# Solving the RWKV-7 chunk systems of a hybrid backbone with 32-row instead of 64-row TensorE tiles, with the products, copies and router reordered to match

## What is computed

```python
def step(state, inp):
    r_t, w_t, k_t, v_t, a_t, b_t = inp
    sa = jnp.einsum('bhvk,bhk->bhv', state, a_t)
    state = (state * w_t[:, :, None, :] + sa[..., None] * b_t[:, :, None, :]
             + v_t[..., None] * k_t[:, :, None, :])
    return state, jnp.einsum('bhvk,bhk->bhv', state, r_t)

for d in range(2):          # forwards, then backwards
    s_ctx, y = rwkv7_scan(r_c, dec, k_d, v_c, -kk_c, kk_c * a, state0, rev)
    _, y = rwkv7_scan(r_l, dec, k_d, v_l, -kk_l, kk_l * a, s_ctx, rev)
...
logits = (h @ w_router).astype(jnp.float32)      # layer 1, before the experts
top_logit, top_idx = lax.top_k(logits, TOP_K)
```

## Time and profile before

| | before |
|---|---|
| median of 3 runs | 2844.2 us (2843.36 to 2848.82) |
| the profiled execution's own time | 2841.97 us |
| its span | 2840.2 us |
| PE busy | 2741.2 us, 97% of the span |
| DVE busy, ACT busy | 1923.5 us (68%), 1524.9 us (54%) |
| the chain that ended last, by engine | PE 90%, DVE 6%, ACT 2%, issue 1% |
| the two scans, from the first D2 stage to the first product behind them | 107.80 to 242.38 us, 1253.40 to 1390.20 us |
| the expert passes | from 1698.5 us on |

### The profile page before, as it was taken

One profiled execution on the slowest core, in us unless ns is written; L12 is line 12 of the kernel. 1 busy time (PEld: TensorE's weight loads), 2 busy tenths in 40 slices (PEclk: granted clock), 3 DMA queues, 4 the chain that ended last, 5 costly groups with the idle time before them and its releaser, 6 DMA issues.

```text
span 2840.2 us, 49672 instructions
## 1 busy us (share of the span) xinstructions
PE 2741.2 (97%) x19396; PEld 2270.1 (80%) x19396; DVE 1923.5 (68%) x2524; ACT 1524.9 (54%) x2045; POOL 0.2 (0%) x4
## 2 busy tenths in 40 slices
PE   7999999999999999899999989999999999999997
PEld 5787777887788888667878988888888888888886
DVE  3766575336322333676656669888898988889897
ACT  5534374223322222543446447777777777777775
POOL 0000000000000000000000000000000000000000
PEclk8999999999999999999999989999999999999998
DMA  6010373224222232201034439999999999999995
GB/s 272 2 47 31 107 267 111 96 100 160 75 104 92 101 123 100 75 1 47 31 134 164 179 153 357 349 346 365 353 360 358 357 348 346 365 353 361 358 357 205
DMA packets 79842, 575.81 MB, mean 203 GB/s; under 512 B 8896, under 2 KB 10176, under 8 KB 10176
## 3 DMA queue, kind: packets, MB, share of 16 engines
q1 hardware_dynamic: 78960, 568.49, 53.1%
q10 hardware_dynamic: 720, 4.99, 0.4%
HBM read 572.39 MB, written 1.05 MB: 202 GB/s over the span
## 4 chain that ended last, share of the span: by engine, by line
PE 90%; DVE 6%; ACT 2%; issue 1%; DMA 0%; DVEq 0%; SPq 0%; ACTq 0%
PE bank L503 88%; ACT arena L1431 1%; PE bank L1339 1%; PE bank L1139 1%; DVE arena L2305 1%; DVE weights_low L1995 1%; DMA xT<-xin 0%; ACT weights_high L1431 0%; PE bank L924 0%; DVE arena L1971 0%; ACT hT L1431 0%; DVE arena L2211 0%; ACT L1431 0%; DVE arena L2091 0%; ACT modT L1431 0%
## 5 line engine op out<-in xcount | busy, mean ns | idle before, releaser
L1431 ACT ACTIVATE weights_high<-ring 128x1024 fp32r<-128x1024 f32 (+1 forms) x366 | 508.8, 1398 | 292.2 <-PE bank L503 291.9
L1431 ACT ACTIVATE arena<-bank 128x256 f32<-128x256 f32 (+7 forms) x581 | 255.6, 455 | 760.7 <-PE bank L503 684.1
L1995 DVE TENSOR_TENSOR weights_low<-ring,weights_high 128x1024 fp32r<-128x1024 f32 x220 | 266.7, 1224 | 403.0 <-ACT weights_high L1431 402.9
L2515 DVE TENSOR_TENSOR weights_low<-ring,weights_high 128x2048 fp32r<-128x2048 f32 x146 | 334.6, 2291 | 69.4 <-ACT weights_high L1431 67.9
L503 PE MATMUL bank<-h_low,weights_high 128*128 128x512 f32 (+1 forms) x960 | 346.8, 361 | 0.0
L503 PE MATMUL bank<-arena 64*64 64x64 f32 (+6 forms) x5168 | 301.2, 246 | 22.5 <-DVE arena L2211 5.8
L503 PEld LDWEIGHTS bank<-arena 64*64 64x64 f32 (+3 forms) x5168 | 252.1, 145 | 48.6 <-issue 17.4
L503 PE MATMUL bank<-weights_high,tokens_high 128*128 128x512 f32 x684 | 271.9, 397 | 1.6 <-DVEq L2538 1.6
L503 PE MATMUL bank<-weights_high,tokens_low 128*128 128x512 f32 x684 | 267.1, 390 | 0.0
L2515 DVE TENSOR_TENSOR more_weights_low<-arena,weights_high 128x2048 fp32r<-128x2048 f32 x108 | 247.4, 2291 | 25.0 <-ACT weights_high L1431 24.8
L1431 ACT ACTIVATE weights_high<-arena 128x2048 fp32r<-128x2048 f32 x108 | 207.0, 1917 | 47.1 <-PE bank L503 47.1
(11 more groups left out here) (294 smaller groups left out, 5348.0 us busy)
## 6 DMA issues: line engine op xcount, KB each, us to landing
ring<-wstream SPq DMA_DIRECT2D x372, 1024.0 KB, 4.8
arena<-wstream SPq DMA_DIRECT2D x167, 1024.0 KB, 4.8
sm<-small ACTq DMA_DIRECT2D x2, 1568.0 KB, 10.4
xT<-xin SPq DMA_DIRECT2D x1, 2048.0 KB, 9.8
cn<-consts ACTq DMA_DIRECT2D x1, 1636.0 KB, 6.6
out<-hT SPq DMA_DIRECT2D x2, 512.0 KB, 3.0
...
```

The lines of the kernel that those rows point to most:

```text
L1431: return nc.scalar.activation(o, i, func, **kw)
L1995: step(vx.tensor_tensor(ring_low[:, u % RING, cols], ring[:, u % RING, cols], wh[:, j % 4, :].bitcast(F32), ALU.subtract), "weights low", j)
L2515: return vx.tensor_tensor(low, raw, moe_high(q).bitcast(F32), ALU.subtract)
```

## The change

- `four` becomes `near`: 16 products (4 heads, 4 blocks of 32) of 32x32 on four diagonal tiles. D2, D4, D8, F2, F3, F4 keep their place and order; D8 is completed on DVE (`D8` add) instead of copied by ACT.
- The rest of a 32-block (mask `cross`) goes in by H and FT (two new products of 32x32), and the coupling of two 32-blocks of one half by one product Z of 32x32 and G1. Z2 and G2 are gone with `last_power`. FC now reads FT and stands behind `carry_y`.
- `carry_u1` multiplies by FT in 32-row tiles, `carry_u` adds the coupling between 32-blocks in the bank where u1's product lies.
- `carry_u0` and `carry_y` go by kinds of product: all from the state, then all from u, then all from v.
- `gram_inner` makes 32 products of 64 rows by 32 columns instead of 16 of 64 by 64.
- ACT: the `exps` of the second direction move between the D4 and F4 copies of groups 1 and 2, with the table load for Exp in group 0; the D2, D4 and F4 copies have 256 columns for each partition, FT 128. DVE: `rates` move to before the F2 add, `hats` split (a, b, k before `carry_state`, r behind G1), and `carry_state` moves ahead of G1.
- Outside the scan: `modulate` writes the first h_high right after the first h; the table for Sqrt is loaded before the squares; the router weights (padded to 32 columns) are the stationary operand in four column tiles, the logits come by a second small product, `first_high(0)` goes before the last `modulate` and `rest(0)` before the logits; the low part of an expert's third unit is made inside the pass.

```diff
+        def leads(d):
+
+            return ((0, 1), (2, 3)) if d == 0 else ((1, 0), (3, 2))
...
-            def four(o, left, right):
+            def near(b, at, left, right):

                 for h in range(4):
-                    for s in range(2):
-                        ins = mm(o[rows(s), h * HD:(h + 1) * HD], left[rows(s), h, :], right[rows(s), h, :])
+                    for t in range(4):
+                        ins = mm(bank[b][blk(t), at + h * BLK:at + (h + 1) * BLK], left[blk(t), h, :], right[blk(t), h, :])
...
-                        mm(bank[6 + p][:, q * HD:(q + 1) * HD], ar_of[d][rows(p), q, c, 0, :], state[rows(p), d, q, :],
-                           True, False)
-                    for p in range(2):
-                        ins = mm(bank[6 + p][:, q * HD:(q + 1) * HD], E1_of[m % 2][:, 2 * p + q, :], vrows(c, p, q), False, True)
-                        if q:
-                            ins.then_inc(*tick(products, "u0 product", l, m, p))
+                        shared(bank[6 + p][:, q * HD:(q + 1) * HD], ar_of[d][rows(p), q, c, 0, :], state[rows(p), d, q, :],
+                               q == 0, False)
+                for p in range(2):
+                    for q in range(2):
+                        ins = shared(bank[6 + p][:, q * HD:(q + 1) * HD], E1_of[m % 2][:, 2 * p + q, :], vrows(c, p, q),
+                                     False, q == 1)
+                    ins.then_inc(*tick(products, "u0 product", l, m, p))
...
-                        def o(p):
-                            return bank[1][rows(p), (2 + q) * P:(3 + q) * P]
                         for p in range(2):
-                            mm(o(p), state[rows(p), d, q, :], ar_of[d][rows(p), q, c, 1, :], True, False)
+                            shared(o(p, q), state[rows(p), d, q, :], ar_of[d][rows(p), q, c, 1, :], q == 0, False)
+                    for q in range(2):
                         for p in range(2):
-                            mm(o(p), uu[:, p, q, :], from_u[:, 2 * p + q, :], False, False)
+                            shared(o(p, q), uu[:, p, q, :], from_u[:, 2 * p + q, :], False, False)
+                    for q in range(2):
                         for p in range(2):
-                            ins = mm(o(p), vrows(c, p, q), from_v[:, 2 * p + q, :], False, True)
+                            ins = shared(o(p, q), vrows(c, p, q), from_v[:, 2 * p + q, :], False, q == 1)
...
-            def last_power(l, n):
-
-                pe.wait_ge(*done("Z2", l, n))
+            def across_second(l, n):
+
+                first, second = ends(groups[n][0])
                 pe.wait_ge(*done("G1", l, n))
-                four(bank[0][:, 256:512], D2[:, 1], FG_of[n % 2][:, 1]).then_inc(*tick(products, "G2 product", l, n))
...
                 if n:
-                    last_power(l, n - 1)
                     carry_u0(l, n - 1)
                     pe.wait_ge(*done("C", l, n))
                 pe.wait_ge(*done("masked D", l, n))
-                four(bank[4][:, 0:256], DD[:, 1], DD[:, 0])
-                four(bank[4][:, 256:512], DD[:, 0], DD[:, 1]).then_inc(*tick(products, "D2 product", l, n))
+                near(5, 0, DT, D)
+                near(5, P, D, DT).then_inc(*tick(products, "D2 product", l, n))
...
-                four(bank[5][:, 256:512], D2[:, 0], D2[:, 1]).then_inc(*tick(products, "D4 product", l, n))
+                near(5, 0, D2[:, 1], D2[:, 0])
+                near(5, P, D2[:, 0], D2[:, 1]).then_inc(*tick(products, "D4 product", l, n))
                 pe.wait_ge(*done("F1", l, n))
-                four(bank[4][:, 256:512], D2[:, 0], FG[:, 0]).then_inc(*tick(products, "F2 product", l, n))
+                near(4, 256, D2[:, 1], F).then_inc(*tick(products, "F2 product", l, n))
...
-                four(bank[4], DD[:, 1], DD[:, 0]).then_inc(*tick(products, "D8 product", l, n))
-                four(bank[5], DD[:, 0], FG[:, 0]).then_inc(*tick(products, "F3 product", l, n))
+                near(5, 0, D4[:, 0], D4[:, 1]).then_inc(*tick(products, "D8 product", l, n))
+                near(4, 256, D4[:, 1], F).then_inc(*tick(products, "F3 product", l, n))
                 if n:
                     carry_across(l, n - 1)
                 pe.wait_ge(*done("D8", l, n))
                 pe.wait_ge(*done("F3", l, n))
-                four(bank[4][:, 256:512], D8, FG[:, 0]).then_inc(*tick(products, "F4 product", l, n))
+                near(4, 256, D8, F)
+                near(4, 384, F, D8).then_inc(*tick(products, "F4 product", l, n))
...
+                pe.wait_ge(*done("F4", l, n))
+                near(5, 0, E16, F4[:, 1]).then_inc(*tick(products, "H product", l, n))
                 if n:
                     carry_state(l, n - 1)
-                pe.wait_ge(*done("F4", l, n))
-                four(bank[5][:, 0:256], EC[:, 0], FG[:, 0])
-                four(bank[5][:, 256:512], FG[:, 0], EC[:, 0]).then_inc(*tick(products, "Z product", l, n))
-                pe.wait_ge(*done("masked k", l, n, 1))
-                across(bank[3], second, FG[:, 0], EC[:, 1], second).then_inc(*tick(products, "FC product", l, n))
+                pe.wait_ge(*done("H", l, n))
+                near(4, 256, F4[:, 0], H).then_inc(*tick(products, "FT product", l, n))
                 if n:
                     carry_y(l, n - 1)
-                pe.wait_ge(*done("Z", l, n))
+                pe.wait_ge(*done("FT", l, n))
+                pe.wait_ge(*done("masked k", l, n, 1))
+                for h in range(4):
+                    for t in range(second.start // BLK, second.stop // BLK):
+                        ins = mm(bank[3][blk(t), h * HD:(h + 1) * HD], FT[blk(t), h, :], EC[blk(t), 1, h, :])
+                ins.then_inc(*tick(products, "FC product", l, n))
                 pe.wait_ge(*done("masked r", l, n))
-                four(bank[0], DD[:, 0], DD[:, 1]).then_inc(*tick(products, "Z2 product", l, n))
+                for h in range(4):
+                    for lead, follow in leads(d):
+                        at = 256 + h * HD + follow % 2 * BLK
+                        ins = mm(bank[0][blk(lead), at:at + BLK], E[blk(follow), h, :], FT[blk(follow), h, :])
+                ins.then_inc(*tick(products, "Z product", l, n))
                 if n < 7:
                     gram_blocks(l, n + 1)

             def scans(l):
                 for n in range(8):
                     solve(l, n)
-                last_power(l, 7)
                 carry_u0(l, 7)
...
-                    if stage and k > some[0]:
+                    if stage and k > some[0] + 1:
                         act.wait_ge(*done("h", l, which, k - 1))
                         h_high(stage, l, k - 1, slice(0, TOK))
+                    if stage and k == some[0]:
+                        act.wait_ge(*done("h", l, which, k))
+                        h_high(stage, l, k, slice(0, TOK))
...
-                    copy(D8, by_head(4), ("D8", "D8 product"), n)
+                    if n in (1, 2):
+                        second_exps(n - 1, 0)
+                        second_exps(n - 1, 1)
+                    if n in (1, 2):
+                        second_exps(n - 1, 2)
...
                 mask_k(l, n, 0)
                 if n:
                     carry_u(l, n - 1)
-                add(l, n, 0, 5, 0, "F3")
+                add(l, n, 4, "F3")
                 if n:
                     carry_across(l, n - 1)
-                add(l, n, 0, 4, 256, "F4")
+                dve.wait_ge(*done("D8 product", l, n))
+                step(vx.tensor_tensor(D8, bank[5][:, 0:P].rearrange("p (h t) -> p h t", h=4), mask("eye32", BLK), ALU.add),
+                     "D8", l, n)
                 mask_k(l, n, 1)
+                if n in (0, 4):
+                    vx.memset(bank[0][:, 256:512], 0.0)
+                dve.wait_ge(*done("H product", l, n))
+                step(vx.tensor_tensor(H, bank[5][:, 0:P].rearrange("p (h t) -> p h t", h=4), mask("eye32", BLK), ALU.add),
+                     "H", l, n)
                 if n < 2:
                     centred_sums(l, 1, n)
                 elif n < 4:
-                    rates(l, 1, n - 2)
-                    hats(l, 1, n - 2)
+                    second_hats(l, n - 2)
                 elif n >= 6:
                     weights_low(LAYER_START[l] + ATT_AT + 2 * n - 10)
-                dve.wait_ge(*done("Z", l, n))
-                step(vx.tensor_tensor(FG_of[n % 2][:, 1], DD[:, 0], mask("eye64"), ALU.add), "G1", l, n)
                 if n:
                     carry_state(l, n - 1)
+                dve.wait_ge(*done("Z product", l, n))
+                step(vx.tensor_tensor(G_of[n % 2], by_head(0, 256), mask("eye64"), ALU.add), "G1", l, n)
+                if n in (2, 3):
+                    step(hat_r(1, n - 2), "hat r", l, n - 2)
                 if n < 7:
...
-                    ins = mm(bank[1 + 6 * t][:, 0:8], hT[:, k, CTX + t * P:CTX + (t + 1) * P], router_w[:, k, :],
-                             k == 0, k == KD - 1)
```

(9 more changed lines are left out.)

221 lines of the change are left out of this document (139 added, 82 removed), and 3 rows, old and new, of the table _n.

## The result

The changed kernel runs in 2883.5 us (median of 4 runs, 2879.8 to 2885.0) against 2843.8 us (2843.1 to 2848.8) of the kernel before on the same chip: ratio 1.0134, 95% interval 1.0119 to 1.0149. That is 38 us slower; 27 us faster was forecast. Its profiled execution has a span of 2878.0 us. The time was lost in the scans; the expert passes are as before to within 1 us.

What follows compares the result with a forecast made beforehand. PE was taken to bound the kernel. Terms of -16.4, -8.0, -1.7, -0.4 and -0.4 summed to -26.9 from 2841.97, 2815.1; stated as 2817 us because the profiled execution was faster than the median, range 2806 to 2828.

Steps and rivals of the forecast that it cites:

- the pace of a wave: Scans: four 32-row products on four tiles take between 0.032 and 0.062 us; 0.032 was taken.
- the dispatch rival: Scans: four records never start in less than 0.062 us, 50 us on top, 2867 us; chance 0.12.
- The clock: Scans: fewer columns in flight and more shape changes drop the clock; one 0.50 stretch in each group gives 2870; chance 0.05.
- Waits: Scans: PE may wait for copies at D4, F4, H and FT, so time comes back, 2831 us; chance 0.18.
- +0.35 a group: Before F4: D8's add queues on DVE behind carry_across's adds, so F4 starts +0.35 us later; bounds +0.6 and 0.
- Order by kinds: Scans, u0 and outputs: ordering products by kind takes four changes of tile shape away, 0.35 x 16 = 5.6 us.
- the 0.33 that I gave the outputs alone: Outputs stage of a group: two changes of tile shape fewer, -0.33 us.
- the -0.15 behind the outputs: Stage from outputs to D2: Z2 and G2 go, FC and Z come, shape changes move; -0.15 us a group.
- Features: Second direction's features in the scans: dealing them out shortens delays and keeps the clock up in layer 1; -8.0 us.
- Norms, start, router: Outside the scans: earlier first h_high -1.7 us, start of the kernel -0.4, router -0.4.
- Router: Router: logits read later, but DVE is rid of rest(0) before the ranks; -0.4 us, bounds +1 and -1.5.
- the solver: Scans: 32-row tiles and changed stages, summed group by group over both layers, together -16.4 us.

Runs made afterwards that it cites:

- the bursts: Kernel before with bursts of small products (32x32 and 64x64) into an unused bank at PE's start, read for its trace alone; 3003.0 us.
- e2_rest: The change without its 32-row tiles: 64-row solver kept, order by kinds, features and edits outside the scans included; 2824.3 us, ratio 0.9922 to the kernel before.
- e5_filler: Changed kernel with three bf16 products of 128x128 by 256 columns added at four places in each group; 2883.6 us, ratio 1.0127 to the kernel before.
- e6_merged: Changed kernel with D4's first 16 products and F2's 16 merged, 64 PE instructions fewer a group, same results; 2866.0 us, ratio 1.0065 to the kernel before.
- e8_spread: e2_rest with 128 useless 32x32 products in each group, 32 at each of four places; 2889.0 us, ratio 1.0151 to the kernel before.
- e3_pairs: Changed kernel with each 32-row product of near() taking two heads at once, halving its instructions, values not the reference's; 2820.6 us, ratio 0.9908 to the kernel before.
- e7_features: Kernel before with only the second direction's features (exps, rates, hats) dealt out as in the change; 2842.3 us, ratio 0.9989.
- e1_order: Kernel before with only carry_u0 and carry_y ordered by kinds of product, 64-row tiles kept; 2842.8 us, ratio 0.9988.

## Why the prediction was wrong, step by step

**The step that failed** is the pace of a wave, "between 0.032 and 0.062 us. I take 0.032". As a pace of the tiles it was good: 24 waves in 1.04 us less one change of shape are 0.039. What it left out is that each of its products is four instructions. A wave of four records with its weight loads is eight, and these arrive in 8 x 3.60 / 256 = 0.112 us, nearly twice the bound that I gave to the dispatch rival. For a group the sum is simple, and all of it was in the trace but the limit: 184 products became some 300, 1215 instructions by the records (x4254 and x4253 in seven groups), which is 4.75 steps of 3.46 to 3.74 us, 16.4 to 17.8 us, where I forecast 14.9 and 13.8. The group shown is longer still, 19.15 us: its packets start 3.5 to 5.2 us apart; PE's other waits come on top, and the next packet starts 1.0 to 2.6 us after PE has gone on, not 1.0 to 1.2 as in the bursts. Before, 729 instructions came in 2.85 steps, 9.9 to 10.6 us, hidden under 16.

**Where the 56 us between e2_rest and the changed kernel are** (spans 2821.7 and 2878.0): 54.9 in the two windows. By stretches of the granted clock:

| kernel | at 1.00: us, per 256 records | at 0.50: us, per 256 records |
|---|---|---|
| after | 178.7, 3.85 | 95.6, 4.80 |
| e5_filler | 217.4, 3.80 | 61.4, 5.81 |
| e6_merged | 178.9, 3.68 | 79.2, 5.55 |
| e8_spread | 266.9, 3.99 | 10.2, 5.83 |

Three kernels with different work in the array take nearly the same for 256 records when the clock is up, 3.68 to 3.85, a little above the steps of the bursts: this is the supply. (e2_rest takes 5.5 for its 256, e3_pairs 4.5.) e8_spread, at 3.99, says less, since its own work would need some 267 of its 277 us (219.4 and 14 x 3.4). The changed kernel's stretches at 0.50 hold 5097 records; at 3.85 for 256 they would take 77 us instead of 96, so about 19 of the 55 us are the clock's. Of the 36 that are left the "issue" gaps account for 26 (29.2 against 3.0 in e2_rest) and the wait ahead of F4 for 5 (10.5 against 5.5). That split is worked out, not shown by a run.

**The rivals.** *Dispatch* (0.12, 2867 us) foretold the right side and nearly the amount by the wrong mechanism: waves at hand stand 0.036 apart and D4 and F2 fell to 1.04 us. It named "groups of the old length without gaps"; there are longer groups with gaps. *The clock* (0.05, 2870 us) is a real second cause. It asked for one 0.50 stretch in each group; there are 11 in the two windows. One of them in layer 1 has no gap by "issue", and there the clock alone sets the pace:

```profile
1304.28:1322.80 18.52, 17.39 (x582) 15.48 (x573) 11.70 (x37) 5.42 (x15) 0.00 (x0) 0.63 0.02 4
1305.14:1318.79 13.65, 13.25 (x402) 12.12 (x389) 8.20 (x26) 4.57 (x13) 0.00 (x0) 0.50 0.02 5
```

What was ahead of the falls: in the bursts, a gap of 4.5 us (the clock fell in it, at 14.9 us, and stayed at 0.50 for the whole 32x32 fp32 burst) and one of 2.5 us (it fell at 90.0 us, just behind it, and stayed down for the bf16 burst), while through the 32x32 products with 64 columns, with gaps of 1.2 to 1.8 us, it stayed at 1.00; in e3_pairs, where gaps are few, narrow products and a wait of 0.9 us before the fall at 160.60 us, one of 1.8 us at that of 170.84. In e2_rest there is none in these windows. What brings the clock down here no run settles. *Waits* (0.18): at F4 PE waits 0.6 to 0.8 us for D8's add against 0.39 before, 5.2 us in layer 0 against 2.9. The forecast had +0.35 a group there, and that was right.

**The other terms.**
- *Order by kinds*, 5.6 us: a group with outputs falls from 15.94 to 15.35 and one without from 14.56 to 14.27, more than the 0.33 that I gave the outputs alone; measured as a whole 3.4 us (0.9 to 6.3). Right in kind and size. The price of a change of shape was read right too: eight records from the state now take 0.59 us up to the next shape (237.78 to 238.37) where four took 0.37, so a pair is 0.11 and the change 0.15. One sum in the list of stages is loose, the -0.15 behind the outputs: with G2 at half its length its parts give +0.06. Without its gap of 1.24 us that stage measures 3.56 us, 0.13 less than before.
- *Features*, 8.0 us: the scans of e7_features are 8.6 us shorter and group 2 of layer 1 keeps its clock, as forecast; the whole measures 3.1 us (0.6 to 5.7). The place was right. Some 5 us went again outside the scans: in its trace 2.7 us from the first scan to the next transposes (115.9 against 113.3) and 1.5 behind the last expert (62.4 against 60.9; e1_order has 62.4 too). The edit touches neither place; why they are longer is open. In the changed kernel itself most of the gain is gone: the same group, from 1322.80 to 1340.70 us, takes 17.90 us, at 0.50 for 6.8 of them.
- *Norms, start, router*, 2.5 us: 6.0 measured (3.4 to 8.5). PE's idle time ahead of the feed-forward fell from 5.67 to 4.83 us, as forecast. The edits also reach the last norm, which I had not counted: from the last expert's transposes to the end e2_rest takes 58.35 us and the kernel before 60.87.

```profile
737.01 0.76 PE L528 MATMUL bank<-h_high_ffn,weights_high 128*128 128x512 f32 x1 [4.83 <-DVE h_low L2084]
```

- *Router*, 0.4 of these 2.5 us (bounds +1 and -1.5): it was mis-sized. DVE's rows from the norm's reciprocal on, before:

```profile
1673.40 1.75 DVE L1971 RECIPROCAL arena<-arena 128x256 f32<-128x256 f32 x1 [1.19 <-ACT arena L1431]
...
1687.40 2.29 DVE L2515 TENSOR_TENSOR weights_low<-ring,weights_high 128x2048 fp32r<-128x2048 f32 x1
1689.61 0.17 DVE L2526 TENSOR_TENSOR rank<-bank,picked 128x16 f32<-128x16 f32 x1
```

 and after:

```profile
1717.20 1.75 DVE L2053 RECIPROCAL arena<-arena 128x256 f32<-128x256 f32 x1 [1.19 <-ACT arena L1485]
...
1721.68 2.28 DVE L2584 TENSOR_TENSOR weights_low<-ring,weights_high 128x2048 fp32r<-128x2048 f32 x1
1726.99 0.17 DVE L2588 COPY logit<-bank 128x16 f32<-128x16 f32 x1 [3.02 <-PE bank L528]
...
1730.93 0.18 DVE L2613 TENSOR_TENSOR rank<-bank,picked 128x16 f32<-128x16 f32 x1
```

 From the reciprocal the logits are read after 9.79 us (before 9.99), not 0.9 later as forecast. The modulation does start 1.7 us later behind the reciprocal (3.97 against 2.25), as I had it; but from there to the logits it takes 5.8 us, where I gave 6.9. And the ranks stand 13.7 us behind it where they stood 16.2, since the first low part (2.3 us) is out of their way. The first expert product starts 21.8 us behind the reciprocal, before 25.1: 3.3 us, not 0.4.

So the parts outside the solver gave together at least what was forecast (22 us against 16.1), though the features alone gave less than half of their term, and the solver, which carried most of the forecast gain (-16.4 us), cost 59 us.
